# VectorE's one-hots made ahead of the next unit's low weights in the scatter stage

## The reference

```python
def peer_block(xb, w_q, sub_keys, expert_u, expert_v):
    q = (xb @ w_q).reshape(T, PEER_HEADS, 2, PEER_HALF)
    s = jnp.einsum('thpd,hpkd->thpk', q, sub_keys)
    sv, si = lax.top_k(s, PEER_TOPK)
    ...
    top_s, pos = lax.top_k(cand, PEER_TOPK)
    eidx = jnp.take_along_axis(cidx, pos, axis=-1)
    gate = jax.nn.softmax(top_s.astype(jnp.float32), axis=-1).astype(xb.dtype)
    u = jnp.take(expert_u, eidx, axis=0)
    act = jax.nn.gelu(jnp.einsum('thkd,td->thk', u, xb))
    v = jnp.take(expert_v, eidx, axis=0)
    return jnp.einsum('thk,thkd->td', gate * act, v)
```

## Time and profile before

| | us |
|---|---|
| median of 3 runs | 2709.02 (2704.39 to 2715.56) |
| the profiled execution's own time | 2700.42 |
| its span | 2699.1 |
| TensorE busy | 2418.8 (90%) |
| VectorE busy | 1926.1 (71%) |
| ScalarE busy | 1002.4 (37%) |
| GpSimd busy | 760.2 (28%) |

### The profile page before, as it was taken

One profiled execution on the slowest core, in us unless ns is written; L12 is line 12 of the kernel. 1 busy time (PEld: TensorE's weight loads), 2 busy tenths in 40 slices (PEclk: granted clock), 3 DMA queues, 4 the chain that ended last, 5 costly groups with the idle time before them and its releaser, 6 DMA issues.

```text
span 2699.1 us, 33461 instructions
## 1 busy us (share of the span) xinstructions
PE 2418.8 (90%) x12402; PEld 2007.4 (74%) x12402; DVE 1926.1 (71%) x3519; ACT 1002.4 (37%) x1686; POOL 760.2 (28%) x512
## 2 busy tenths in 40 slices
PE   7989988988888898989899899799877889999997
PEld 5768988988888887989888887588544577545555
DVE  7899889886777777988989996643467645155554
ACT  3332333333333332323333334422356524244443
POOL 4010444440111125767777771200000020000001
PEclk9999999999999998989999999899899999999999
DMA  6446444445777679999999993111000012100001
GB/s 239 178 166 248 140 137 140 138 142 204 251 256 251 245 270 367 374 342 346 364 367 357 365 358 129 55 60 58 32 1 1 17 55 78 57 23 13 18 1 63
DMA packets 162225, 465.93 MB, mean 173 GB/s; under 512 B 15504, under 2 KB 72976, under 8 KB 159632
## 3 DMA queue, kind: packets, MB, share of 16 engines
q1 hardware_dynamic: 100368, 304.40, 31.5%
q0 software_dynamic: 36864, 134.23, 13.6%
q10 hardware_dynamic: 24832, 25.17, 2.9%
HBM read 411.31 MB, written 52.43 MB: 172 GB/s over the span
## 4 chain that ended last, share of the span: by engine, by line
PE 57%; DVE 23%; DMA 8%; issue 7%; ACT 4%; POOL 1%; DVEq 0%; ACTq 0%
PE psum L412 5%; PE psum L413 5%; PE psum L414 5%; PE psum L420 5%; PE psum L422 4%; PE psum L421 4%; DVE weights_low L1347 4%; PE psum L524 4%; DMA arena<-in_v_rows,arena 3%; DMA arena<-in_u_rows,arena 2%; DVE arena L1544 2%; PE psum L836 2%; PE psum L438 2%; DVE arena L1530 2%; DMA arena<-hidden 2%
## 5 line engine op out<-in xcount | busy, mean ns | idle before, releaser
L1347 DVE TENSOR_TENSOR weights_low<-arena,weights_high 128x1024 fp32r<-128x1024 f32 x290 | 401.6, 1385 | 273.5 <-ACT weights_high L913 271.4
L913 ACT ACTIVATE weights_high<-arena 128x1024 fp32r<-128x1024 f32 x355 | 374.6, 1055 | 425.8 <-PE psum L553 285.5
L551 PE MATMUL psum<-hidden_high,weights_high 128*128 128x384 f32 x1024 | 353.5, 345 | 58.5 <-DVE hidden_low L1574 51.2
L420 PE MATMUL psum<-x_high,weights_high 128*128 128x384 f32 x1024 | 357.8, 349 | 36.3 <-POOL weights_low L1861 29.4
L421 PE MATMUL psum<-x_low,weights_high 128*128 128x384 f32 x1024 | 349.1, 341 | 0.0
L422 PE MATMUL psum<-x_high,weights_low 128*128 128x384 f32 x1024 | 349.0, 341 | 0.0
L553 PE MATMUL psum<-hidden_high,weights_low 128*128 128x384 f32 x1024 | 347.5, 339 | 0.0
L552 PE MATMUL psum<-hidden_low,weights_high 128*128 128x384 f32 x1024 | 347.2, 339 | 0.0
L412 PE MATMUL psum<-x_high,weights_high 128*128 128x512 f32 (+1 forms) x696 | 277.4, 399 | 25.3 <-DVE weights_low L1347 20.4
L413 PE MATMUL psum<-x_low,weights_high 128*128 128x512 f32 (+1 forms) x696 | 272.3, 391 | 0.0
L414 PE MATMUL psum<-x_high,weights_low 128*128 128x512 f32 (+1 forms) x696 | 272.1, 391 | 0.0
(11 more groups left out here) (237 smaller groups left out, 4295.5 us busy)
## 6 DMA issues: line engine op xcount, KB each, us to landing
arena<-in_stream SPq DMA_DIRECT2D x227, 512.0 KB
arena<-in_v_rows SPq DMA_DIRECT2D x128, 512.0 KB
arena<-in_ada_w SPq DMA_DIRECT2D x48, 512.0 KB, 3.3
hidden<-arena SPq DMA_DIRECT2D x128, 192.0 KB, 3.5
router<-arena SPq DMA_DIRECT2D x12, 2048.0 KB
arena<-hidden SPq DMA_DIRECT2D x128, 192.0 KB
arena<-router ACTq DMA_DIRECT2D x16, 1536.0 KB
arena<-in_pair_w SPq DMA_DIRECT2D x8, 576.0 KB, 3.7
```

What stands on the lines that cost most here:

```text
L420: PE.matmul(bank[b][:, 0:N], wh[u % 2][:, k, :], xh[:, k, PICKED:T], start=k == 0, stop=False)
L551: PE.matmul(out, wh[w][:, n, :], hh[:, r, :], start=e == 0, stop=False)
L913: ACT.activation(wh[u % 2], slots[u % RING], AF.Copy).then_inc(*tick("weights_high", u))
L1347: DVE.tensor_tensor(wl[u % 2], slots[u % RING], wh[u % 2].bitcast(F32), ALU.subtract).then_inc(*tick("weights", u))
```

## The change

On each of VectorE's steps the one-hots are moved ahead of the low weights. No instruction is added or removed, and no other engine's order changes.

```diff
         DVE.wait_ge(*at("entered", 2))
         for n in range(1, KEYS - UNDER_ROUTER):
-            low_weights(unit("up", UNDER_ROUTER + n) + 1)
             for i in range(quads_before(n - 1), quads_before(n)):
                 one_hots(i)
+            low_weights(unit("up", UNDER_ROUTER + n) + 1)
             for j in ROWS_AT["up", n]:
                 use_row(j)
```

## The result

| | before | changed |
|---|---|---|
| first series: median | 2706.7 us (4 runs) | 2632.9 us (4 runs), 2628.8 to 2636.1 |
| ratio | | 0.9721, 95% interval 0.9694 to 0.9748 |
| second series, another set of runs: median | 2701.8 us (17 runs) | 2636.8 us (5 runs) |
| ratio | | 0.9759, 0.9734 to 0.9783 |
| profiled execution: span | 2699.1 us | 2634.8 us |

The forecast was 2648 us, with a range of 2634 to 2668. The measured 2632.9 of the first series lies 1 us under the range and 15 us under the forecast.

A forecast was written before the change was run, and what follows sets the result against it. It took a closed loop through TensorE, ScalarE and VectorE to bound the scatter stage. Gains of 31.9 and 30.0 us, taken as 60, gave 2700.4 - 60 = 2640, plus the median offset, less 1: 2648 us; range 2634 to 2668.

The forecast's parts named there:

- The loop: Scatter stage: scatter, staging, high weights, low weights, one-hots close a 5.70 us loop; a second quad makes it 7.33.
- rival D: Scatter stage: waits called "issue" are TensorE's own, so no change, 2709 us; chance 3%.
- "issue" is VectorE: Before 92 of 96 scatters, the wait labelled "issue" is really a wait for VectorE's one-hots.
- TensorE's step: Scatter stage: without waits, an up unit and its scatters take 5.13 us, or 6.01 with two quads.
- 2 off for the first steps: Scatter stage: 1 to 2 us taken off the 61.9 us sum because the first steps settle, leaving 60.
- The scale of the result: Whole kernel: the profiled execution lies 8.6 us under the median, so 2640 us becomes 2649 as a median.
- likeliest case: The forecast itself, chance 80%: range 2636 us (62 gained, profiled scale) to 2667 (42 gained, median's scale).
- Low weights, queues, what follows: Scatter stage and later: later low weights have 2 us slack, queues cost about 0, following stages shift as a whole.
- Rival B: Scatter stage: each GpSimd issue holds VectorE 0.94 us on 51 steps; gain about 44 us, 2665 us; chance 10%.
- the rule on GpSimd: Shared SBUF port pair: VectorE or GpSimd, whichever starts first, blocks the other for its whole instruction; issues lengthen towards 1.5 us.
- C: Scatter stage: GpSimd's issue stretches two one-hot instructions a step, +1.34 us each; 44 us lost, 2753 us; chance 2%.
- E: DMA gives gain back: 12 stores each hold ScalarE 2 us, down stage's entry loses 5; 2678 us; chance 5%.

The follow-up runs named there:

- doubled hot1: Each quad's hot1 made twice, the second copy unused: 2657.7 us in the changed kernel; 2771.0 us, ratio 1.0252, in the kernel before.
- half change: Changed kernel with only the first quad's one-hots ahead of the low weights, the second's behind: 2632.7 us, ratio to before 0.9744.
- two repeated profiles: Profiles from rerunning both kernels without edits: kernel before against itself 2698.6 us, ratio 0.9993; changed kernel again, ratio 0.9759 to before.
- row-first kernel: Changed kernel with the gathered row also ahead of the low weights (one-hots, row, low weights): 2632.1 us, ratio to before 0.9728.
- version with more rows: Changed kernel with 21 gathered rows moved from the down stage into the scatter steps: 2611.2 us, ratio to before 0.9659.

## Why the prediction was right, and what it mis-sized

**The loop: right.** The path through ScalarE and the second quad's 1.63 us were read from the trace alone. That six times add up to exactly 5.70 us is no proof, though the prediction takes it for one against rival D: each is the distance from one start to the next, so between two scatters they must add up to the distance of the scatters. What speaks for a loop in these rows is that no hop has slack: the staging, the low weights and the scatter each start as soon as what they wait for is done, with waits of 0.98, 1.70 and 0.40 us in front of them. The runs are the proof. The doubled hot1 showed it twice, 68 us inside the loop and 21 outside, and the half change showed that a loop shorter than TensorE's step costs nothing.

**"issue" is VectorE: right.** The label stood before 92 of 96 scatters and all are gone, with nothing on TensorE changed.

**TensorE's step: mechanism right, size off by 4 us.** The prediction took 0.88 us for a quad's pieces, from the earlier trace rows, and made steps of 5.13 and 6.01. They are 5.06 and 5.94. The 0.88 us were measured behind a gap, each time; without a gap eight pieces take 0.81 (747.31 to 748.12) and sixteen 1.70 (741.37 to 743.07). So each step gained 0.07 us more than forecast, 56 x 0.07 = 4 us., which the prediction quotes, had said so: 16 pieces in 1.70, 0.106 each, is 0.85 for eight. The last piece of the last scatter starts at 925.3 us instead of 991.6, 66 us earlier; the span gained 64.3, the down stage having become 2.6 us longer (in the two repeated profiles it took 615.2 before and 614.2 changed, so this is within what it varies). The prediction's sum was 61.9, from which it took 2 off for the first steps; nothing was lost there.

**The scale of the result: wrong, and this step failed.** The prediction added 8.6 us because the median shown stood that far above the profiled execution. That offset does not belong to the changed kernel, nor to the one before: over 17 runs of the second series before has a median of 2701.8, 1.4 us above the profiled 2700.4. The changed kernel's profiled execution, 2636.1 us, was the longest of its four, 3.2 above their median. The 15.1 us from the forecast to the median are these: 4.3 for a gain of 64.3 instead of 60, 8.6 for the offset, 3.2 for the place of the profiled execution among four, less the 1 us that the prediction had taken off. The 3.2 are chance. So is the side of the range's edge: the first series lies 1 us outside, the second, 2636.8, inside. Without the offset the prediction's own sum gives 2639 to 2640.

Two more figures of the range do not hold. A gain of 62 us from 2700.4 is 2638.5, not the 2636 that the prediction gives as its likeliest case's low end. And with 2634 it left 4 us beyond its sum on that side and 28 on the other. By medians the first series shows 73.8 us, but 64 to 66 by its profiles and by the second series: some 9 us of the 73.8 are which executions fell into its four and four.

Where executions differ can be seen. The stretch from the last down unit to the last instruction takes 1046 to 1049 us in seven of the nine profiles (1586.8 to 2634.8 in the changed kernel's), 1065.6 in the row-first kernel's and 1065.7 in that of the version with more rows. The difference lies in 200 us of an attention behind the down stage. The same stretch, in the changed kernel and in the row-first kernel (windows):

```profile
1886.80:2086.80 200.00, 157.59 (x965) 95.28 (x966) 137.97 (x403) 123.46 (x379) 0.00 (x0) 0.97 0.00 1
```

```profile
1882.20:2082.20 200.00, 161.47 (x892) 91.52 (x892) 127.83 (x383) 113.39 (x360) 0.00 (x0) 0.86 0.00 1
```

The granted clock is 0.97 in one and 0.86 in the other, and 965 matmuls stand in the first against 892. In the version with more rows the stretch (1867 to 2067 us) has 0.86 and 892 too. The scatter stage has 1.00 in both. So one execution can be 17 us longer than another of the same kernel, and a median of three carries that. What makes the clock drop in some executions was not tried.

**Low weights, queues, what follows: right at cost nothing.** TensorE never waits for line 1347 in the scatter steps; no gelu waits there for a hidden store, and the stages behind moved nearly as a whole (45.0 and 613.9 us before, 45.0 and 616.5 now). In the last up units gelu does wait for hidden stores, 16.7 us in all, but it did before, 13.9. That these stages run at the pace of their transfers is not shown (above).

**Rival B, and the rule on GpSimd.** GpSimd's issues now fall on the one-hots, as expected, but they do not lengthen towards the 1.5 us that the prediction named. They take 1.15 us, where they took 0.94 in VectorE's idle time (the changed kernel, 640 to 926 us; minimum/median/maximum in ns):

```profile
L1870 POOL DMA_INDIRECT arena<-in_u_rows,arena x30: 936/1146/1148, 639.0 to 923.9; - x30
L1870 POOL DMA_INDIRECT arena<-in_v_rows,arena x21: 1141/1145/1147, 690.9 to 918.2; - x21
```

The one-hots took 689 ns for line 1555 and 346 for one of line 1558 in the median, against 685 and 342 before, and at most 445:

```profile
L1555 DVE TENSOR_TENSOR arena<-con,arena x96: 683/689/702, 607.6 to 919.4; 128x512 f32<-128x512 f32 x96
L1558 DVE TENSOR_SCALAR arena<-con,arena x384: 337/346/445, 608.2 to 920.8; 128x128 f32<-128x128 f32 x192
```

VectorE is held by 0.1 us at most, not by the 0.94 of B. The Trainium skill (SBUF — State Buffer, "SBUF: two separate sides") gives the shared ports as an exclusive lock for a whole instruction, if VectorE's instruction is in a two-port mode, or has two inputs in SBUF and GpSimd's reads SBUF. The prediction left this condition out, and no run here tells whether the one-hots meet it. What the runs show is an issue lengthened by 0.2 us beside one-hots, and in no scatter stage an instruction of VectorE that was longer by more than 0.1 us. C had nothing for it and D fell with the gaps. E did not come: DMA went to a share of 0.82 without a late scatter.

## What to carry to other kernels

When an engine's waits repeat with one period, follow them back from release to release. If the path comes back to the same engine one period earlier, and on every hop the next instruction starts as soon as its releaser is done, a loop sets the pace and no single engine does. Taking one piece of work out of the loop then pays its full length, until the loop is shorter than the busiest engine's own step. The sum of the hops alone proves nothing, as it comes out by construction; work added inside and outside the loop does. On an in-order engine that piece is often one that only stands behind another's wait: put what is ready ahead of what is not. And take the sum from the profiled execution's own time; add an offset to a median only when many runs show it.

## What the hardware showed that was not expected

- In the kernel before with hot1 made twice, TensorE's granted clock falls to its lower level nine times in the scatter stage (0.97 over the stage); the gaps before its scatters are mostly 1.0 to 1.1 us. In the kernel before, with gaps of 0.4 to 0.5 us, it stays at 1.00.
- A group of eight 128x128 float32 pieces on TensorE takes 0.88 us behind a gap of 0.4 us and 0.81 without, at a granted clock of 1.00 in both.
- The length of an indirect issue on GpSimd goes with what VectorE runs when it starts: 0.94 us beside an idle VectorE, 1.15 beside the one-hots, and 1.68 to 2.28 beside the low weights and what follows them. Row-first kernel, 640 to 926 us, issues of `expert_v` rows, of which some fall into idle time:

```profile
L1870 POOL DMA_INDIRECT arena<-in_v_rows,arena x22: 936/1696/2283, 686.4 to 923.9; - x22
```
